# Mixture of experts: rows turned by VectorE in 32x32 squares, and the down matrix loaded by four transfers of 32 partitions

## The reference

```python
x  = x + g1 * m                                   # m: the mixers' output @ w_out
h2 = rmsnorm(x, norm_ffn_w) * (1.0 + sc2) + sh2
grp = argmax(h2 @ router_g_w + router_g_b)        # one of 4 groups
top_v, top_i = top_k(e_logits[grp], 2)            # two of its 8 experts, e_logits = h2 @ router_e_w + b
gates = p_grp * softmax(top_v)
# every chosen row, by expert, in blocks:
hdn = silu(xb @ w_gate[e]) * (xb @ w_up[e])       # 1024 -> 512
y   = (hdn @ w_down[e]) * gate                    # 512 -> 1024
x = x + g2 * sum of a row's two y
y = rmsnorm(x, final_norm_w)
```

## Time and profile before

| | |
|---|---|
| timed runs, us | 3000.09, 2998.96, 3000.0 (median 3000.0) |
| span of the profiled execution, us | 3002.4 (81057 instructions) |
| TensorE busy | 2798.6 us, 93% |
| VectorE busy | 1423.0 us, 47% |
| ScalarE busy | 888.2 us, 30% |
| GpSimd busy | 416.7 us, 14% |
| DMA | 580.55 MB, mean 193 GB/s |
| mean granted TensorE clock | 0.969 |

### The profile page before, as it was taken

One profiled execution on the slowest core, in us unless ns is written; L12 is line 12 of the kernel. 1 busy time (PEld: TensorE's weight loads), 2 busy tenths in 40 slices (PEclk: granted clock), 3 DMA queues, 4 the chain that ended last, 5 costly groups with the idle time before them and its releaser, 6 DMA issues. The chain is left out here.

```text
span 3002.4 us, 81057 instructions
## 1 busy us (share of the span) xinstructions
PE 2798.6 (93%) x33765; PEld 1640.7 (55%) x33766; DVE 1423.0 (47%) x3553; ACT 888.2 (30%) x1898; POOL 416.7 (14%) x633
## 2 busy tenths in 40 slices
PE   6998999999999989999998799958999999999988
PEld 3432445455454557887787455524555555555543
DVE  3246356555566647777777344561222222222218
ACT  2347244344344434444444122210000000000006
POOL 0000000000000001121123000003222222222223
PEclk8999999999999989999999799979999999999999
DMA  8641124223232396556553785555896588768858
GB/s 296 217 142 43 50 86 136 74 106 119 99 127 107 119 252 162 161 156 183 160 151 90 242 295 196 218 202 183 302 336 252 202 303 310 282 247 297 293 198 341
DMA packets 377451, 580.55 MB, mean 193 GB/s; under 512 B 56526, under 2 KB 240774, under 8 KB 374184
## 3 DMA queue, kind: packets, MB, share of 16 engines
q1 hardware_dynamic: 327176, 486.12, 47.2%
q0 software_dynamic: 18832, 70.53, 6.7%
q10 hardware_dynamic: 31248, 21.08, 2.4%
HBM read 412.03 MB, written 165.60 MB: 192 GB/s over the span
## 5 line engine op out<-in xcount | busy, mean ns | idle before, releaser
L523 PE MATMUL pj_P<-normed,pj_wc 128*128 128x448 f32 (+2 forms) x1600 | 594.8, 519 | 0.9 <-ACT pj_stage L656 0.9
L2714 PE MATMUL moe_PG<-wgu,moe_xT 128*32 128x256 f32 x9600 | 550.7, 381 | 0.0
L523 PEld LDWEIGHTS pj_P<-normed,pj_wc 128*128 128x128 f32 x1600 | 295.8, 190 | 259.5 <-issue 243.6
L2714 PEld LDWEIGHTS moe_PG<-wgu,moe_xT 128*32 128x32 f32 x9600 | 297.0, 110 | 206.6 <-issue 26.8
L2544 DVE TENSOR_TENSOR moe_sg<-moe_sg,moe_PG 128x128 f32<-128x128 f32 x150 | 43.1, 288 | 556.0 <-ACT moe_sg L2593 556.0
L2725 PE MATMUL moe_PTY<-wd,moe_hT 128*32 128x256 f32 x4800 | 286.5, 379 | 0.6 <-DVE moe_hT L2549 0.6
L2593 ACT ACTIVATE moe_sg<-moe_PG 128x128 f32<-128x128 f32 x150 | 41.8, 278 | 793.3 <-PE moe_PG L2714 793.3
L2132 PE MATMUL merge_PO<-merge_w,merge_mT 128*128 128x512 f32 x544 | 240.0, 599 | 0.6 <-ACT merge_mT L2178 0.6
L2725 PEld LDWEIGHTS moe_PTY<-wd,moe_hT 128*32 128x32 f32 x4800 | 155.9, 110 | 103.5 <-DVE moe_y L2537 0.7
L2132 PEld LDWEIGHTS merge_PO<-merge_w,merge_mT 128*128 128x128 f32 x544 | 102.7, 191 | 125.1 <-issue 124.4
L2636 POOL DMA_INDIRECT moe_xg<-scratch_h,moe_row x154 | 149.9, 974 | 125.7 <-POOL moe_xc L2649 114.9
(11 more groups left out here) (434 smaller groups left out, 4231.6 us busy)
## 6 DMA issues: line engine op xcount, KB each, us to landing
wgu<-in_w_gate SPq DMA_DIRECT2D x32, 2048.0 KB
wgu<-in_w_up SPq DMA_DIRECT2D x32, 2048.0 KB
wd<-in_w_down SPq DMA_DIRECT2D x32, 2048.0 KB
scratch_y_rows<-merge_zeros SPq DMA_DIRECT2D x51, 512.0 KB, 4.8
scratch_hk<-pj_hk SPq DMA_DIRECT2D x16, 1344.0 KB, 5.8
normed<-scratch_hk SPq DMA_DIRECT2D x32, 640.0 KB, 7.9
re_hkf<-scratch_hk SPq DMA_DIRECT2D x32, 640.0 KB
scratch_y_rows<-moe_y ACTq DMA_DIRECT2D x604, 32.0 KB
```

The lines of the kernel that those rows point to most:

```text
L523: ins = eng.matmul(bank[:, 0:wp], wc[:, j, k, :], hT[:, k, k0:k0 + wp], start=(k == 0), stop=(k == KD - 1), skip_group_check=True)
L2714: ins = eng.matmul(PG[32 * q:32 * q + 32, 0, 0:256].rearrange("p (a b) -> p a b", a=2), x_rows, wgu[p][:, :, k, 128 * q:128 * q + 128], st ...
```

## The change

The gathered rows and the hidden rows are no longer turned by TensorE. VectorE has a transpose that turns each 32x32 square of a tile by itself, from SBUF to SBUF; it takes `xg[p]` to `xT` and `hid` to `hT`. What such a transpose puts on one partition is not what the 128x128 transpose does, so the order of the stored data changes:

- h2 is written to memory with its 1024 features in the order (q, k, a) where it was (k, q, a), with 4 q, 8 k and 32 a; then partition 32 q + a of square k has feature 128 k + 32 q + a, and w_gate and w_up stay as they are. In `merge` the first half of h2's formula goes into the buffer of x, and the second writes h2 in the new order; the load of a later x into that buffer waits for it.
- The router's weights are loaded in the matching order, by 40 transfers where there were 5.
- The hidden features lie on the partitions in another order too, so the down matrix is loaded by four transfers, each to 32 partitions with its 128 rows taken 32 apart.

TensorE's `turn` and `turn_hid`, ScalarE's copy of `xT`, GpSimd's copy to `xc` and the PSUM tile of the turned rows are gone. VectorE turns block g + 1 right after gate_up(g) is done and before it multiplies for block g; it turns the hidden rows after `keep_y`. GpSimd's next gather into `xg[p]` waits for VectorE's transpose. gate_up waits for `x_turned` and for the hidden rows of the block before, which read the same PSUM tile.

```diff
# load_expert
+        src = t[("w_gate", "w_up", "w_down")[n]][0, ds(e, 1)]
+        if n < 2:
+            eng.dma_start(gate_up[:, n, :, :], src.rearrange("e (k p) n -> p (e k) n", p=128)).then_inc(loaded[n], 16)
+        else:
+            for q in range(4):
+                rows = src[:, 128 * q:128 * q + 128, :].rearrange("e (j a) n -> a (e j) n", a=BLOCK)
+                eng.dma_start(down[BLOCK * q:BLOCK * q + BLOCK, :, :], rows).then_inc(loaded[n], 16)
# experts, VectorE
+                def turn_x(g, p, turned):
+                    eng.wait_ge(ev(f"gathered{p}"), turned * 16 + 16)
+                    eng.transpose(xT[:, :, :].rearrange("p k r -> p (k r)"), xg[p][:, :]).then_inc(ev("x_turned"), 1)
+                turn_x(0, 0, 0)
                 with eng.Fori(0, n_pairs) as i:
                     for p in range(2):
                         g = i * 2 + p
+                        eng.wait_ge(ev("gu_made"), g + 1)
+                        turn_x(g + 1, 1 - p, i + p)
                         eng.wait_ge(ev("sigmoid_made"), g + 1)
...
                         keep_y(g + 1, 1 - p, i)
-                        eng.wait_ge(ev("h_turned"), g + 1)
-                        eng.tensor_copy(hT[:, :], PH[:, 0, 0:128]).then_inc(ev("hT_kept"), 1)
+                        eng.wait_ge(ev("hid_ready"), g + 1)
+                        eng.transpose(hT[:, :], hid[:, :]).then_inc(ev("hT_kept"), 1)
# experts, ScalarE
-                        eng.wait_ge(ev("x_turned"), g + 3)
-                        eng.copy(xT[:, :, :], PT[:, :, :]).then_inc(ev("xT_kept"), 1)
# experts, GpSimd
+                        eng.wait_ge(ev("row_ready"), i * 2 + (p + 3))
                         eng.wait_ge(ev("x_turned"), i * 2 + (p + 1))
-                        eng.sem_inc(ev("move_begun"), 1)
-                        eng.tensor_copy(xc[:, :], xg[p][:, :]).then_inc(ev("x_moved"), 1)
-                        eng.wait_ge(ev("row_ready"), i * 2 + (p + 3))
-                        eng.wait_ge(ev("x_moved"), i * 2 + (p + 1))
                         gather(p)
# experts, TensorE
-                    for k in range(2):
-                        ins = eng.transpose(PT[:, k, :], xc[:, 128 * k:128 * k + 128], ident)
-                    ins.then_inc(ev("x_turned"), 1)
-                    eng.transpose(PH[:, 0, 0:128], hid[:, :], ident).then_inc(ev("h_turned"), 1)
+                    if not first:
+                        eng.wait_ge(ev("hid_ready"), g)
+                    eng.wait_ge(ev("x_turned"), g + 1)
...
-                        turn(g + 1)
-                        turn_hid(g - 1)
                         gate_up(g, p)
                         down(g, p)
...
-                    eng.wait_ge(loaded[p][2], i * 16 + 16)
+                    eng.wait_ge(loaded[p][2], i * 64 + 64)
# merge, VectorE
-                step(eng.scalar_tensor_tensor(h2[:, p, :], x1[:, p, :], stat[:, 3:4], m[:, 1, :], ALU.mult, ALU.mult))
+                step(eng.scalar_tensor_tensor(x[:, p, :], x1[:, p, :], stat[:, 3:4], m[:, 1, :], ALU.mult, ALU.mult))
...
-                eng.tensor_tensor(h2[:, p, :], h2[:, p, :], m[:, 2, :], ALU.add).then_inc(ev("h2_ready"), 1)
+                to = h2[:, p, :].rearrange("p (q k a) -> p k q a", q=4, k=KD)
+                eng.tensor_tensor(to, pieces(x[:, p, :]), pieces(m[:, 2, :]), ALU.add).then_inc(ev("h2_ready"), 1)
# merge, SyncE
+                eng.wait_ge(ev("h2_ready"), at(i, 2, n + 1))
                 if not (i is None and n + 2 > NT - 1):
                     load_x(i, n + 2)
-                eng.wait_ge(ev("h2_ready"), at(i, 2, n + 1))
# recur, SyncE: 5 transfers of the router weights become 40
+            for j in range(4):
+                to = held["wr"][32 * j:32 * j + 32, :, :].rearrange("a (q k) n -> a q k n", q=4)
+                of = [w.rearrange("(k j q a) n -> j a q k n", k=2, j=4, q=4)[j] for w in (t["router_g_w"][0], *(t["router_e_w"][0, g] for g in range(N_GROUPS)))]
+                for k in range(2):
+                    eng.dma_start(to[:, :, k, 0:N_GROUPS], of[0][:, :, k, :]).then_inc(held_in, 16)
+                    for g in range(N_GROUPS):
+                        c = N_GROUPS + PER_GROUP * g
+                        eng.dma_start(to[:, :, k, c:c + PER_GROUP], of[1 + g][:, :, k, :]).then_inc(held_in, 16)
```

More of the change, by code:

```diff
@@ L1971 @@
 NR = N_GROUPS + N_EXPERTS
-N_SMALL = 4 + N_GROUPS
+N_SMALL = 3 + 8 * (1 + N_GROUPS)
 D_EXPERT = 512
@@ L1987, in load_expert @@
     for n in matrices:
-        src = t[("w_gate", "w_up", "w_down")[n]][0, ds(e, 1)].rearrange("e (k p) n -> p (e k) n", p=128)
-        eng.dma_start(gate_up[:, n, :, :] if n < 2 else down[:, :, :], src).then_inc(loaded[n], 16)
+        src = t[("w_gate", "w_up", "w_down")[n]][0, ds(e, 1)]
[5 more added lines that the diff above has]
+                eng.dma_start(down[BLOCK * q:BLOCK * q + BLOCK, :, :], rows).then_inc(loaded[n], 16)
 def merge(nc, t, expert, gates, wgu, wd, loaded, held, held_in, tables):
@@ L2235, in restart, with pieces @@
                 count = 0
+            def pieces(x):
+                return x.rearrange("p (k q a) -> p k q a", k=KD, q=4)
             def norm(i, n):
@@ L2368, in experts @@
         xg = [sb(f"xg{p}", [128, 256]) for p in range(2)]
-        xc = sb("xc", [128, 256])
-        xT = sb("xT", [128, 2, 128])
+        xT = sb("xT", [128, KD, BLOCK])
         sg = sb("sg", [128, 128])
@@ L2583, in store_y @@
                     eng.sem_inc(ev("store_begun"), 1)
-                n_blocks = total(eng)
-                eng.wait_ge(ev("x_turned"), 1 + 1)
-                eng.copy(xT[:, :, :], PT[:, :, :]).then_inc(ev("xT_kept"), 1)
-                n_pairs = n_blocks // 2
+                n_pairs = total(eng) // 2
                 with eng.Fori(0, n_pairs) as i:
@@ L2593, in _ @@
                         eng.activation(sg[:, :], PG[:, 0, 0:128], ACT.Sigmoid).then_inc(ev("sigmoid_made"), 1)
-                        eng.wait_ge(ev("x_turned"), g + 3)
-                        eng.copy(xT[:, :, :], PT[:, :, :]).then_inc(ev("xT_kept"), 1)
                         store_y(g, 1 - p)
                 store_y(n_pairs * 2, 1)
-                eng.wait_ge(ev("xT_kept"), n_pairs * 2 + 1)
                 eng.wait_ge(ev("y0_out"), n_pairs * 64 + 64)
@@ L2641, in _ @@
                     gather(p)
-                n_pairs = (n_blocks + 2) // 2
+                n_pairs = n_blocks // 2
                 with eng.Fori(0, n_pairs) as i:
@@ L2667, in _ @@
                 eng.wait_ge(ev("member_ready"), 1)
-                for name in ("x_turned", "y_made", "y_kept"):
+                for name in ("y_made", "y_kept"):
                     eng.sem_inc(ev(name), 1)
@@ L2692, in _, with gate_up @@
                 eng.wait_ge(ev("rows_ready"), 1)
-                def turn(g, first=False):
-                    eng.wait_ge(ev("x_moved"), g + 1)
+                def gate_up(g, p, first=False):
                     if not first:
-                        eng.wait_ge(ev("xT_kept"), g)
-                    for k in range(2):
-                        ins = eng.transpose(PT[:, k, :], xc[:, 128 * k:128 * k + 128], ident)
-                    ins.then_inc(ev("x_turned"), 1)
-                def turn_hid(g):
-                    eng.wait_ge(ev("hid_ready"), g + 1)
-                    eng.transpose(PH[:, 0, 0:128], hid[:, :], ident).then_inc(ev("h_turned"), 1)
-                def gate_up(g, p):
-                    eng.wait_ge(ev("xT_kept"), g + 1)
+                        eng.wait_ge(ev("hid_ready"), g)
+                    eng.wait_ge(ev("x_turned"), g + 1)
                     for k in range(KD):
-                        x_rows = xT[:, k % 2, 32 * (k // 2):32 * (k // 2) + 32]
                         for q in range(4):
-                            ins = eng.matmul(PG[32 * q:32 * q + 32, 0, 0:256].rearrange("p (a b) -> p a b", a=2), x_rows, wgu[p][:, :, k, 128 * q:128 * q + 128],
+                            ins = eng.matmul(PG[32 * q:32 * q + 32, 0, 0:256].rearrange("p (a b) -> p a b", a=2), xT[:, k, :], wgu[p][:, :, k, 128 * q:128 * q + 128],
                                              start=(k == 0), stop=(k == KD - 1))
@@ L2748, in next_expert @@
                     down(g, 1 - p)
-                    eng.wait_ge(loaded[p][2], i * 16 + 16)
+                    eng.wait_ge(loaded[p][2], i * 64 + 64)
                     eng.sem_inc(ev("down_begun"), 1)
-                turn(0, first=True)
                 before, first, second = blocks_of_pair(eng, 0)
-                for matrix in range(3):
+                for matrix in range(2):
                     eng.wait_ge(loaded[0][matrix], 16)
-                eng.wait_ge(ev("xT_kept"), 1)
-                turn(1)
-                gate_up(before, 0)
+                eng.wait_ge(loaded[0][2], 64)
+                gate_up(before, 0, first=True)
                 rest_of_expert(before, first, 0)
@@ L2768, in _ @@
                 n_blocks = total(eng)
-                turn_hid(n_blocks - 1)
```

1 line of the change is left out of this document (removed).

## The result

| us | before | after |
|---|---|---|
| timed runs, median (lowest to highest) | 3000.1 (2998.96 to 3004.82) | 2981.7 (2969.86 to 2992.77) |
| span of the profiled execution | 3002.4 | 2979.5 |
| first gate/up matmul to the end of that span | 2036.5 to 3002.4: 965.9 | 2035.9 to 2979.5: 943.6 |
| mean granted TensorE clock | 0.969 | 0.964 |

The ratio after/before is 0.9929, 95% interval 0.9911 to 0.9947. The forecast was 2942 us. It lies outside what was measured; the direction and the range held. Nearly all of the difference between the spans, 22.3 of 22.9 us, lies in the experts' stage (the third row).

A forecast was written before the change was run, and what follows sets the result against it. It took TensorE's unbroken chain in the experts' stage, 5.80 us a block for 150 blocks, as the bound, DMA engines second. Terms -80 + 25 - 3 = -58 on 3002.4 gave 2944.4, less 2.4: 2942 us; range 2904 to 2990.

The forecast's parts named there:

- Transposes leave TensorE, -80: Experts' stage: three transposes a block leave TensorE's chain, saving 72 to 87 us, 80 taken.
- the bound of 87: Upper end of the transposes' saving, by matmul starts: a block of 5.22 us, 0.58 saved, 150 blocks.
- The branch for which 7 us were held back: TensorE has to branch once a block; 80 us of saving was taken where 87 was the upper end.
- VectorE's transposes, 0: Experts' stage: VectorE's transposes cost 0 at about 0.42 us, free up to about 0.97 us; bounds 0 to 107 us.
- Rival 3: Experts' stage: VectorE's transpose, at 1.5 us, takes the place of TensorE's; no change, 2997 us; chance 0.08.
- The gather, 0: Experts' stage: gathers, issued later, have 9.2 us to land and take at most about 6.8; cost 0.
- The down matrix in four transfers, +25: Experts' stage: down loads at 219 GB/s take 9.6 us instead of 5.9; TensorE waits 25 us; bounds 0 to 182.
- this branch (31 to 36 us): TensorE's waits for down loads if gathers and stores take their 18% from the narrow transfers; otherwise 12 to 16 us.
- rival 2: Experts' stage: down loads become the bound, at 142 GB/s costing 81 to 182 us; slower, 3056 us; chance 0.08.
- Start of the stage, -3: First block's gate and up wait for one VectorE transpose instead of two on TensorE: -3 us.
- Router weights and merge, 0: 35 more SyncE transfers, up to 30 us, stay hidden (upper bound 5); merge's later x load and permuted write cost 0.
- rival 1: Experts' stage: the narrow down loads don't matter; -90 us, 2910 us; chance 0.13.

The follow-up runs named there:

- wide loads: The changed kernel with w_down loaded by one transfer of 128 partitions in plain order, the permutation moved into gate/up's moving operand: 2916.7 us, ratio 0.9705.
- one edit: Against the kernel with one down transfer of 128 partitions: that transfer made four of 32 partitions, rows in plain order; 2976.8 us, ratio 0.9919.

## Why the prediction was wrong, point by point

- **Transposes leave TensorE, -80:** right. A steady block saves 0.62 us, 93 us in all, above the bound of 87: the 5.22 us came from starts in the old block, where 64 matmuls of gate and up took 3.48 us between transposes; they take 3.45 now. By the chain it was 3.59 us there, so the 0.10 us that the prediction added to the transposes' own 0.48 are 0.14. The branch for which 7 us were held back costs nothing within a pair of experts. At the end of a pair it shows, in waits ("issue" 7.1 us in 17 waits with wide loads, against 2.9 in 14 before), 4 us, and in the 18 pieces of 3.66 us, 0.21 x 18, another 4 us. That leaves 93 - 8 = 85; between the stages before and with wide loads 965.9 - 881.5 = 84.4 us were measured. That 80 came so near is in part luck: the saving of a block was taken too small and the cost of the branch put in the wrong place.
- **VectorE's transposes, 0:** right: 0.445 us for 128x256, beside sigmoid, and 0.30 us for 128x128. Rival 3 is out.
- **The gather, 0:** wrong in a part. The lead of 9.2 us was right, but its 6.8 us of landing was read in a stretch of wide loads. Behind narrow ones it lands after 10.18 and 11.19 us, and VectorE waits for it 34.2 us, of which TensorE gets a few (3.9 - 1.3 = 2.6 us by "moe_hid", and perhaps some of what stands under "issue"). With wide loads there is at most one such wait, of 4 us.
- **The down matrix in four transfers, +25:** this is the step that failed. It cost 62 us between the stages of after and of the wide kernel (943.6 - 881.5), 65 us between their times, and 60 us as one edit (2916.7 to 2976.8). The rate taken, 219 GB/s, was right: 222 measured. But that is what the full engines move on average with gathers and stores included. The prediction had this branch (31 to 36 us) and took a value between it and the other; TensorE's waits named w_down for 31.6 us. Of these 28 stand at two of the places that were forecast, after the experts of three blocks (2170 to 2283 us, and 2540 to 2570); at the end, the third place, there are 1.2. The sum turned a rate into waits for w_down alone, and the rest are costs which it did not have: the same delay reaches gate and up of the next expert (5.4 us); the waits under "issue" grow from 7.1 to 11.5 us; and TensorE runs its first work after a long wait at half clock. By windows of 2 us, 34 us of the stage were at the lower level in after, none before or with wide loads; they hold up to 17 us lost. So of 62 us between the stages, 57.5 - 13.4 = 44 are waits, some 3 the pieces of 3.66 us after 14 more waits (33 against 19), and the 15 that remain fit the clock.
- **The rates:** the rule that the prediction cited against the change (the Trainium skill, SBUF — State Buffer, "Can I just issue two DMAs to hit both halves?") agrees with the runs, 222 of about 400 GB/s. What was priced too low is what hangs on it. With 16 partitions it was the same: 172 GB/s were measured where rival 2 took 142, and yet the price, 3108.0 - 2916.7 = 191 us, lies above its 81 to 182.
- **Start of the stage, -3:** from transpose to first gate/up is now 0.5 us (2035.41 to 2035.91) where it was 3.0: right. **Router weights and merge, 0:** right as far as the runs can tell; the 40 transfers took 23.7 us on SyncE, and its load was still in time.
- **The sum by what was measured:** -93 + 8 + 62 = -23 for the stage, where -22.3 was measured. The 15 us of the clock in the 62 are what the other terms leave, not a reading of their own.
- **The rivals:** rival 1 (narrow loads don't matter, 2910) is near the wide kernel's time, 2916.7, reached only by taking the narrow loads out; as a forecast it is refuted. Rival 2's mechanism is the one at work; at 32 partitions it takes two thirds of the saving, and at 16 its sign: 3108 us.

## What to carry to other kernels

When a change makes a load narrower, count its cost at every wait of the stage, and not only at its own: the rate of the narrow transfer is shared by all that is in the queues, so gathers behind it land late too, and TensorE pays again in clock after each long wait. Look for the permutation that can be put into an operand that is read anyway (here the moving operand in runs of 32 columns, at no cost) before it is put into a DMA. And a piece of the chain can be worth more than its length when the engine changes its tile for it: the smallest piece, 0.11 us, was worth 0.40.

## What the runs showed of the hardware

- Full DMA engines moved 172, 222, 224 and about 400 GB/s with transfers to 16, 32, 64 and 128 partitions among their traffic; 64 was no better than 32. The rows of w_down are of 4 KB in all of them.
- SyncE's issue of one load of w_up took 0.53 us, and up to 10.49 us while the loads issued before it were still under way.
- After TensorE had waited 3.96 us, gate and up took 5.35 us at a mean granted clock of 0.68 of 2.4 GHz; after 1.23 us, 3.66 us at full clock.
- VectorE's transpose in 32x32 squares of float32 took 0.445 us for 128x256, a copy of 128x256 from PSUM 0.425 us.
- One 128x128 transpose between groups of 128x32 matmuls made a block 0.40 us longer (5.58 against 5.18), and two more beside it 0.22 (5.80 against 5.58).
- A moving operand of 256 columns in strided runs of 32 float32 columns took the time of the plain one, 3.45 us for 64 matmuls.
